# Dummy matmuls between the pieces of the first attention's steps

## The reference

```python
q, k, v, iq, ik, iw = split(x @ w_in)                 # 16 query heads, 4 key/value heads, 64 wide
q, k = partial_rotary(q), partial_rotary(k)
logits = einsum('bqgrd,bqkgd->bqgrk', q_b, k_sel) * 64 ** -0.5
p = softmax(where(valid, logits, -inf))
o = einsum('bqgrk,bqkgd->bqgrd', p, v_sel)
out = o.reshape(1, 256, 1024) @ w_o
```

## Time and profile before

| what | value |
|---|---|
| median of the runs | 1397.33 us |
| the profiled execution's own time | 1394.16 us |
| its span, first to last instruction | 1392.3 us |
| mean granted TensorE clock over the span | 0.967 |
| TensorE busy | 1326.4 us (95%), 10604 matmul records |
| VectorE busy | 928.1 us (67%) |
| ScalarE busy | 627.4 us (45%) |
| float32 dummies of line 497 | 464 records, mean 275 ns of one |

### The profile page before, as it was taken

How to read it: one execution, slowest core, us unless ns; L and a number is a source line. 1 busy time by engine, 2 the same in 40 slices (tenths; PEclk the granted TensorE clock), 3 DMA queues, 4 the chain that set the end, 5 groups by cost and what they waited for, 6 DMA issues and landing times.

```text
span 1392.3 us, 25125 instructions
## 1 busy us (share of the span) xinstructions
PE 1326.4 (95%) x10604; PEld 1272.3 (91%) x10604; DVE 928.1 (67%) x1448; ACT 627.4 (45%) x805; POOL 0.2 (0%) x4
## 2 busy tenths in 40 slices
PE   6889999999998899999999999999899999999897
PEld 6866999999998799999999999889898989999797
DVE  6783576466647767646665458888876665999943
ACT  5334454354444244534435444454445455555431
POOL 0000000000000000000000000000000000000000
PEclk9975999999999899999999999999999999999999
DMA  8320325545334133554532543334445241444430
GB/s 330 115 91 0 122 104 198 184 178 191 115 122 152 61 121 105 198 184 179 195 138 94 209 159 120 118 127 150 141 172 203 92 152 61 152 181 157 175 121 31
DMA packets 28361, 198.41 MB, mean 142 GB/s; under 512 B 3296, under 2 KB 3808, under 8 KB 4592
## 3 DMA queue, kind: packets, MB, share of 16 engines
q1 hardware_dynamic: 27072, 194.00, 38.7%
q10 hardware_dynamic: 1200, 3.14, 0.6%
HBM read 196.08 MB, written 1.05 MB: 142 GB/s over the span
## 4 chain that ended last, share of the span: by engine, by line
PE 69%; DVE 23%; ACT 3%; issue 3%; DMA 1%; DVEq 0%; ACTq 0%
PE lin L422 19%; PE lin L424 18%; PE lin L423 18%; DVE wlo L1307 7%; DVE conv L1748 3%; PE lin L504 2%; PE att L589 2%; PE att L497 2%; DVE fconv L1922 1%; PE att L556 1%; ACT whi L906 1%; PE att L573 1%; DVE fconv L1921 1%; DVE fconv L1923 1%; PE lin L527 1%
## 5 line engine op out<-in xcount | busy, mean ns | idle before, releaser
L422 PE MATMUL lin<-xh,whi 128*128 128x256 f32 x1936 | 556.2, 287 | 17.2 <-DVE xl L1317 11.8
L1307 DVE TENSOR_TENSOR wlo<-raw,whi 128x2048 fp32r<-128x2048 f32 x183 | 418.7, 2291 | 215.2 <-ACT whi L906 214.0
L423 PE MATMUL lin<-xl,whi 128*128 128x256 f32 x1936 | 550.8, 284 | 0.0
L424 PE MATMUL lin<-xh,wlo 128*128 128x256 f32 x1936 | 550.5, 284 | 0.0
L906 ACT ACTIVATE whi<-raw 128x2048 fp32r<-128x2048 f32 x183 | 348.5, 1906 | 179.5 <-PE lin L424 172.7
L422 PEld LDWEIGHTS lin<-xh,whi 128*128 128x128 f32 x1936 | 375.0, 194 | 21.4 <-DVE wlo L1307 10.6
L423 PEld LDWEIGHTS lin<-xl,whi 128*128 128x128 f32 x1936 | 375.0, 194 | 0.1
L424 PEld LDWEIGHTS lin<-xh,wlo 128*128 128x128 f32 x1936 | 374.5, 193 | 0.0
L422 PE MATMUL lin<-fh,whi 128*128 128x256 f32 x512 | 143.4, 280 | 0.0
L423 PE MATMUL lin<-fl,whi 128*128 128x256 f32 x512 | 142.8, 279 | 0.0
L424 PE MATMUL lin<-fh,wlo 128*128 128x256 f32 x512 | 142.8, 279 | 0.0
(11 more groups left out here) (309 smaller groups left out, 1645.5 us busy)
## 6 DMA issues: line engine op xcount, KB each, us to landing
raw<-units_dram SPq DMA_DIRECT2D x183, 1024.0 KB, 4.8
h<-x_dram SPq DMA_DIRECT2D x1, 1024.0 KB, 6.8
memT<-mem_dram ACTq DMA_DIRECT2D x1, 1024.0 KB, 4.8
out_dram<-h SPq DMA_DIRECT2D x4, 256.0 KB, 2.0
consts<-consts_dram ACTq DMA_DIRECT2D x1, 867.5 KB, 12.2
narrow_a<-narrow_a_dram ACTq DMA_DIRECT2D x1, 544.0 KB, 14.1
vec<-vectors_dram ACTq DMA_DIRECT2D x1, 245.5 KB, 16.9
posi<-pos_dram ACTq DMA_DIRECT2D x1, 128.0 KB, 8.0
```

Of the source, the lines that this page charges most:

```text
L422: mm(out, w[0], a[0], start=first, stop=False)
L423: mm(out, w[0], a[1], start=False, stop=False)
L424: return mm(out, w[1], a[0], start=False, stop=last)
L1307: v.tensor_tensor(wlo[u % RING][:], raw[u % RING][:], whi[u % RING][:].bitcast(f32), ALU.subtract).then_inc(lo_ready, 1)
```

## The change

`keep_warm` gets an argument for the place it writes to. `att_step` gets a function that it calls between L and T, and again between T and V. Only the first attention passes one. There, the dummies write into the `lin` bank of the first job of the output projection, and 12 of them stand ahead of step 0. In steps 0 to 3 each call issues 7 dummies, in steps 4 to 18 each call issues 4. So 12 + 4 x 14 + 15 x 8 = 188 dummies are added. The other engines' programs stay as they are.

```diff
-            def keep_warm(n):
+            def keep_warm(n, out=None):
 
                 for _ in range(n):
-                    mm(att[0][:, 0:P], ident, ident, start=True, stop=True)
+                    mm(att[0][:, 0:P] if out is None else out, ident, ident, start=True, stop=True)
...
-            def att_step(s, u0, n):
+            def att_step(s, u0, n, between=None):
                 if s < n:
                     att_logits(u0 + s)
+                if between:
+                    between()
                 if 2 <= s < n + 2:
                     att_transpose(u0 + s - 2)
+                if between:
+                    between()
                 if 3 <= s < n + 3:
                     att_values(u0 + s - 3)
...
             pe.wait_ge(kswapped, 2)
             evacuated(pe, JOB["v", 0])
+            idle = bank(JOB["ao", 0])[:, 0, 0:P]
+            keep_warm(12, idle)
             for s in range(16 + 3):
-                att_step(s, ATT0["A"], 16)
+                att_step(s, ATT0["A"], 16, lambda: keep_warm(7 if s < 4 else 4, idle))
             keep_warm(9)
             ups("ao", "ao")
```

## The result

The changed kernel takes 1411.84 us (median of 4, from 1410.19 to 1411.97) against 1396.43 us before in the same comparison: ratio 1.0112, 95% interval 1.0100 to 1.0124. It is slower by 15.4 us. Run once more beside other kernels it gave 1410.88 us, ratio 1.0105 (1.0088 to 1.0122).

What follows compares the result with a forecast made beforehand. The prediction took TensorE at half clock to bound the first attention. Opening +8.2, steps 4 to 15 +0.5 and end +4.5 gave +13.2 us: 1407.4 profiled, 1410.5 with the median's 3.2 offset; range 1403 to 1424, own range 1403.7 to 1418.5.

Steps and rivals of the forecast that it cites:

- TensorE is the bound of this stage, at half its pace: First attention: TensorE busy 10.00 of 10 us at clock 0.50, its pieces L, T, V alone making the 3.88 us step.
- Full clock holds: First attention: with dummies the clock stays full, as TensorE is never idle and much time goes to full 128 x 128 work.
- falling-clock rival: First attention: the clock falls despite the dummies, a step takes 7.49 us, +62 us in all, 1460 us; chance 9%.
- Dummies cost what the clock gives back: Steps 4 to 15: eight dummies almost cancel the clock's gain, 3.92 us a step instead of 3.88, +0.5 us.
- Opening +8.2: Up to step 4: 68 dummies plus pieces at full clock start step 4 at 101.99 instead of 93.75, +8.2 us.
- End +4.5: Steps 16 to 18: 24 dummies, 2 T and 3 V take 8.55 us instead of 4.06, +4.5 us.
- Transposes gain from the clock: First attention's T: 0.83 us at half clock, 0.48 at full; without that gain the sum would be +18.8 us.
- Keeping TensorE busy as a sufficient condition: Cited advice that a TensorE busy without pause has full throughput; the forecast said a window at clock 0.50 contradicts it.
- Nothing comes back later: Output projection and later stages stay as they are, hiding no added length; the opposing rival, +0, about 1397 us, had 2%.
- Overlap: Rival in the first attention: dummies run beside half-filled L and V, saving 24.2 us, -11 in all, 1386 us; chance 4%.

Runs made afterwards that it cites:

- e3_opening: Changed kernel with dummies only ahead and in steps 0 to 3 (12, then 7 per gap), none later, 68 added: 1381.73 us, ratio 0.9894 to the kernel before.
- e7_narrow: Changed kernel with no dummies after step 3 and each of the 68 added ones over 64 partitions instead of 128: 1383.43 us, 0.9908 of the kernel before.
- e10_burst_narrow: Changed kernel with only 12 added dummies, all in step 4, each over 64 partitions: 1400.84 us, ratio 1.0026 to the kernel before.
- e8_fit_no_tail: Changed kernel with 4 dummies ahead, 3 per gap in steps 0 to 3, none later, the nine old ones left out: 1375.06 us, 0.9846 of before.
- e1_half: Changed kernel with 3 dummies per gap in steps 0 to 3 and 2 later, 96 added: 1389.04 us, ratio 0.9954 to the kernel before.
- e2_one: Changed kernel with 3 dummies per gap in steps 0 to 3 and 1 later, 66 added: 1382.76 us, ratio 0.9899 to the kernel before.
- e5_fit: Changed kernel with 4 dummies ahead, 3 per gap in steps 0 to 3, none later, 28 added: 1375.73 us, ratio 0.9860 to the kernel before.
- e9_burst: Changed kernel with only 12 added full dummies, 6 in each gap of step 4: 1379.35 us, ratio 0.9873 to the kernel before.
- e6_ahead: Changed kernel with only the 12 dummies ahead of step 0, none between the pieces: 1396.59 us, ratio 1.0004 to the kernel before.
- e4_later: Changed kernel with no dummies ahead or in steps 0 to 3, 4 per gap from step 4, 120 added: 1403.58 us, 1.0050 of the kernel before.

## Why the prediction was right

The forecast was +13.2 us, 1410.5; measured +15.4, 1411.84, with +14.8 us in the stage itself. That 1410.5 came within 1.3 us of 1411.84 is partly luck. It was 1407.4 for the profiled execution plus 3.2 us by which the kernel before's median lay above its profiled execution. The changed kernel's profiled execution took 1411.80, as long as its median. Profile against profile the change is +17.6 us, and the stage's +14.8 is the part that the sum was about.

- *TensorE is the bound of this stage, at half its pace.* Right: in steps 4 to 15, where e3_opening and the kernel before issue the same instructions, a step takes 2.13 us at clock 1.00 instead of 3.88 at 0.50.
- *Full clock holds.* Right, 1.00 all through. Of the two reasons given, that TensorE is never idle was enough; that much of its time goes to full 128 x 128 work was not needed, as e3_opening (no dummies from step 4 on) and e7_narrow (half-height ones) keep full clock too. The falling-clock rival is refuted for this kernel. It named a real danger in the wrong place: half-filled work does not lose full clock here, it only fails to regain it.
- *Dummies cost what the clock gives back.* Right: 3.96 instead of 3.88 us a step, forecast 3.92. Taken apart by e3_opening, a step without dummies is 2.13 (the sum had 2.00), and the eight dummies with their two gaps are 3.96 - 2.13 = 1.83 (the sum had 1.80). The 3.92 was chosen between two bounds, so that it lay this near is in part chance.
- *Opening +8.2:* measured +9.0. *End +4.5:* measured +4.9. Both terms were a little small, for two reasons. I took 0.226 us a dummy everywhere; inside a row it is that, but a change between dummies and pieces adds to it: the opening's 68 dummies took 2.77 + 2 x 3.32 + 4 x 1.66 = 16.05 us, not 15.3. And V takes 0.80, not 0.725, L 0.85, not 0.79; T, between dummies, takes 0.33, less than 0.48, which gives part of it back.
- *Transposes gain from the clock.* Right, against the rule of the Trainium skill that the prediction cites (TensorE: Matmul & The Clock Gate, Part 4: PE-mode transpose): T takes 0.47 in e3_opening against 0.83, in the same order of instructions and with the clock at 1.00 instead of 0.50. The measurement decides.
- *Keeping TensorE busy as a sufficient condition*, the prediction's other citation of the Trainium skill (same page, "Why this matters for your kernels"), was refuted by the kernel before, and e10_burst_narrow refutes it once more: busy 10 of 10 us, clock 0.50.
- *Nothing comes back later.* Right, with one detail that I had not seen: the nine dummies behind the attention stand in a wait of 1.9 us (e8_fit_no_tail). For the change it plays no part as far as the traces show: VectorE's split starts 1.2 us behind the last V in the changed kernel (160.87, V up to 159.69) as in the kernel before (145.54, V up to 144.37).
- *Overlap.* Right that it does not happen with full dummies; e7_narrow shows that it does with half-height ones.

What the prediction did not ask is whether all 188 dummies were needed. 28 are enough, ahead of and in the first four steps; fewer in the opening were not tried.

## What to carry to other kernels

Where a busy TensorE runs at half clock, look for the idle time at which the clock fell, and fill that; do not thicken the steady work behind it, which here kept full clock by itself. Dummies that lay in a wait were free here, dummies in a stage that TensorE bounds cost their full time: 0.229 us each in the changed kernel, 0.233 in e1_half and 0.255 in e2_one, gaps included (the step less 2.13, by their number). So count them against what the clock can give back. To regain a lost clock, one burst of full-size matmuls was worth 17 us here, but the wait is better filled in the first place (21 us).

## What the runs showed that I had not expected

The same sequence of scores, transposes and value products ran steadily at either level: at 0.50 for 54 us in the kernel before, at 1.00 in e3_opening, e5_fit and e9_burst, and stayed where it was found. Twelve dummies over 128 partitions moved it up, twelve over 64 did not (e9_burst, e10_burst_narrow). Twelve full dummies placed before the wait did not prevent the fall (e6_ahead), a wait of 0.95 us did not cause one (e5_fit). In e4_later waits of 0.95 and 0.81 us close together were all that stood in the attention ahead of the fall. So it is shown that filling the opening's waits prevents it, and not which of them causes it.
